# Seven block products for eight blocks of each FFN: gate weight sums on VectorE, up weight sums on GpSimd

## What is computed

```python
D_MODEL = 1024
SEQ = 512
D_FF = 2816

def swiglu_ffn(x, gain, w_gate, w_up, w_down):
    h = rms_norm(x, gain)
    return (jax.nn.silu(h @ w_gate) * (h @ w_up)) @ w_down
```

## Time and profile before

| | |
|---|---|
| median of 3 runs | 1033.64 us (1031.59 to 1034.01) |
| span of the profiled execution | 1029.8 us |
| PE busy | 1020.8 us, 5674 matmuls |
| PEld busy | 841.4 us |
| DVE busy | 545.6 us |
| ACT busy | 367.5 us |
| POOL busy | 386.1 us |
| PE clock granted | 0.999 |
| HBM read | 92.16 MB |

### The profile page before, as it was taken

The page is one execution under the profiler, slowest core; times in us unless marked ns, Lnnn a source line. Parts: engine busy times, 40 slices in busy tenths (PEclk is TensorE's granted clock), DMA queues, the critical chain, the costliest instruction groups (busy, mean ns, idle before and its releaser), DMA issues.

```text
span 1029.8 us, 14318 instructions
## 1 busy us (share of the span) xinstructions
PE 1020.8 (99%) x5674; PEld 841.4 (82%) x5674; DVE 545.6 (53%) x839; ACT 367.5 (36%) x503; POOL 386.1 (37%) x97
## 2 busy tenths in 40 slices
PE   9999999999999999999999999999999999999998
PEld 7878888888888888788877888888888888888887
DVE  5593344433444477862557884784333443344435
ACT  7533213222132243444356664632321322213220
POOL 0164433434434431533252201526353443443440
PEclk9999999999999999999999999999999999999999
DMA  8333222232232221231221001313323223222212
GB/s 320 126 123 122 82 101 103 81 119 85 81 118 86 89 115 41 88 117 41 83 78 48 3 2 41 123 41 123 123 81 116 87 81 122 81 88 116 81 41 82
DMA packets 15734, 94.80 MB, mean 92 GB/s; under 512 B 2000, under 2 KB 2128, under 8 KB 5456
## 3 DMA queue, kind: packets, MB, share of 16 engines
q1 hardware_dynamic: 15696, 94.27, 25.4%
HBM read 92.16 MB, written 2.10 MB: 92 GB/s over the span
## 4 chain that ended last, share of the span: by engine, by line
PE 91%; DVE 4%; DMA 1%; issue 1%; ACT 1%; POOL 1%; SPq 1%; POOLq 0%; DVEq 0%
PE bank L1497 83%; DMA raw<-stream 1%; POOL wlo L387 1%; PE bank L1851 0%; DVE prob L1255 0%; PE bank L1855 0%; DVE rowmax L1257 0%; PE bank L1899 0%; ACT sqx L477 0%; DVE alo L874 0%; PE bank L1782 0%; PE bank L1965 0%; PE bank L1877 0%; PE bank L1801 0%; PE bank L1954 0%
## 5 line engine op out<-in xcount | busy, mean ns | idle before, releaser
L387 POOL TENSOR_TENSOR wlo<-raw,whi 128x2048 fp32r<-128x2048 f32 x80 | 370.1, 4629 | 548.0 <-ACT whi L452 534.7
L1497 PE MATMUL bank<-ahi,whi 128*128 128x512 f32 x944 | 370.6, 393 | 2.2 <-POOL wlo L387 2.2
L1497 PE MATMUL bank<-ahi,wlo 128*128 128x512 f32 x944 | 367.7, 389 | 0.0
L1497 PE MATMUL bank<-alo,whi 128*128 128x512 f32 x944 | 367.4, 389 | 0.0
L452 ACT ACTIVATE whi<-raw 128x2048 fp32r<-128x2048 f32 x80 | 152.6, 1912 | 339.9 <-PE bank L1497 315.9
L1497 PEld LDWEIGHTS bank<-ahi,whi 128*128 128x128 f32 x944 | 177.2, 188 | 42.5 <-POOL wlo L387 2.6
L1497 PEld LDWEIGHTS bank<-ahi,wlo 128*128 128x128 f32 x944 | 177.2, 188 | 37.1
L1497 PEld LDWEIGHTS bank<-alo,whi 128*128 128x128 f32 x944 | 177.3, 188 | 35.9
L1017 DVE SCALAR_TENSOR_TENSOR x<-bank,x 128x512 f32<-128x512 f32 x176 | 120.9, 690 | 83.8 <-PE bank L1497 83.2
L1497 PE MATMUL bank<-hhi,whi 128*128 128x512 f32 x352 | 137.2, 390 | 0.0
L1497 PE MATMUL bank<-hlo,whi 128*128 128x512 f32 x352 | 137.0, 389 | 0.0
(11 more groups left out here) (277 smaller groups left out, 739.1 us busy)
## 6 DMA issues: line engine op xcount, KB each, us to landing
raw<-stream SPq DMA_DIRECT2D x80, 1024.0 KB, 4.7
raw<-stream SPq DMA_DIRECT2D x6, 512.0 KB, 6.5
x<-x_in SPq DMA_DIRECT2D x4, 512.0 KB, 7.2
out<-x SPq DMA_DIRECT2D x8, 256.0 KB, 2.0
raw<-stream SPq DMA_DIRECT2D x4, 256.0 KB, 6.5
memx<-mem_in SPq DMA_DIRECT2D x2, 512.0 KB, 10.6
cst<-const_in SPq DMA_DIRECT2D x1, 480.0 KB, 7.3
cst<-const_in SPq DMA_DIRECT2D x1, 256.0 KB, 5.7
```

What stands on the lines that cost most here:

```text
L387: nc.gpsimd.tensor_tensor(wlo[:, u % RING, :], raw[:, u % RAW, :], whi[:, u % RING, :].bitcast(F32), ALU.subtract).then_inc(w_lo, 1)
L1497: ins = E.matmul(dst, a, b, start=(n == 0 and i == 0), stop=(n == last and i == 2))
```

## The change

The first three blocks of each FFN (CLASSIC = 3) stay as they were; the other eight (FAST = 8, `i` from 0 to 7, called bodies here) get gate and up by seven products. The 1024x256 weight block is cut into four blocks of 512x128, and the input into four blocks of 512 channels x 256 tokens. Each of gate and up is then seven products (items q = 0 to 13 of a body; 0 to 3 gate, 4 to 7 up, 8 to 10 gate, 11 to 13 up) of 4x3 = 12 matmuls with 256 moving columns. Down is as before, 48 matmuls of 512 columns.

What comes with it:

- Input side, once per FFN, during the three classic blocks: DVE writes the normalized x (`normalize`, 8 instructions of 128x512), four differences (`t_total`, 128x1024) and six low parts (`t_low`, 128x1024); ACT seven high parts (`t_high`, 128x1024); POOL one low part. Three pairs of the operands lie in the place of `ahi` and `alo` and are written only once the last classic up unit is through.
- Weight side, per body: the sums of weight blocks are one add of 128x1024 and two of 128x512 for gate on DVE (`weight_sums`) and the same for up on POOL (`up_sums`). ACT makes 18 high pieces of 128x512 in groups of one to four (`pieces_high`), POOL 14 low pieces of 128x512 one at a time (`piece_low`), DVE the four low pieces of the down unit as one instruction of 128x2048 (`down_low`). The rings are used as 12 slots of such pieces.
- Output side, per body: for gate and up each, ACT copies 128x256 out of PSUM (`p6_copy`), DVE makes three combinations of 128x256 (`combine`) before the last three products and two (`fix`) after them. The scaling by the norm is gone from the bodies, since the input is normalized.
- Waits: item 8 waits for `combine` of gate and item 11 for `combine` of up (`c22_done`); the DMA of a body's gate weights waits for low piece 10 of the body before, that of its up weights for piece 13, that of its down weights for `down_low`. `weight_sums` of the next body stands between the two `combine` on DVE (in body 0 behind both).
- The loops are written out. In the mixing part, `weight_hi(U_IN + 1)` on ACT moves from before `x_parts(1)` to behind it. In FFN1, ACT makes the high part of unit v+1 before the first silu, and DVE the second half of the first hidden block behind the memory sums.

```diff
+            def first_four(f, i, g):
+                q, xb, yb = 4 * g, 2 * g, 2 * g + 1
+                seventh(f, i, q, T_B11, xb, 0, True, g == 0 and i > 0)
+                seventh(f, i, q + 1, T_1, yb, 0, True, False)
+                seventh(f, i, q + 2, T_3, yb, 1, False, False)
+                seventh(f, i, q + 3, T_2, xb, 1, False, False, four_done)
+            def last_three(f, i, g):
+                q, xb, yb = 8 + 3 * g, 2 * g, 2 * g + 1
+                pe.wait_ge(c22_done, 2 * (FAST * f + i) + g + 1)
+                seventh(f, i, q, T_B21, xb, 0, False, False, x_bank_done)
+                seventh(f, i, q + 1, T_4, yb, 1, False, False)
+                seventh(f, i, q + 2, T_B22, yb, 0, False, False, y_bank_done)
...
+                for i in range(FAST):
+                    h = n0 + 2 * (i + CLASSIC)
+                    if i == 0:
+                        pe.wait_ge(gate_scaled, 2 * CLASSIC * (f + 1))
+                    else:
+                        pe.wait_ge(silu_done, h)
+                    first_four(f, i, 0)
+                    pe.wait_ge(h_done, h)
+                    first_four(f, i, 1)
+                    last_three(f, i, 0)
+                    last_three(f, i, 1)
+                    pe.wait_ge(f_down_lo, (FAST + 1) * f + i + 1)
+                    pe.wait_ge(h_lo, h)
+                    fast_down(f, BODY * i + 14, (i + CLASSIC - 1) % 2, d0 + KD * (i + CLASSIC - 1))
```

DVE, classic part and bodies:

```diff
+                hidden(f, 0)
+                normalize(f)
+                gate_scale(f, 1)
+                t_total(f, T_1)
+                t_total(f, T_3)
+                t_low(f, T_B11)
+                t_low(f, T_1)
+                ffn_add(d0, 0)
+                ffn_add(d0, 1)
+                hidden(f, 1, low=False)
+                for d in range(2, KD):
+                    ffn_add(d0, d)
+                hidden_low(f, 1)
+                t_low(f, T_3)
+                weight_sums(f, 0, 0)
+                gate_scale(f, 2)
+                t_total(f, T_2)
...
+                t_total(f, T_4)
+                hidden(f, 2, low=False)
+                t_low(f, T_B21)
+                ffn_add(d0 + KD, 4)
+                ffn_add(d0 + KD, 5)
+                t_low(f, T_B22)
+                ffn_add(d0 + KD, 6)
+                ffn_add(d0 + KD, 7)
+                t_low(f, T_4)
+                hidden_low(f, 2)
+                for i in range(FAST):
+                    before = d0 + KD * (i + CLASSIC - 1)
+                    combine(f, i, 0)
+                    if 0 < i < FAST - 1:
+                        weight_sums(f, i + 1, 0)
+                    combine(f, i, 1)
+                    if i == 0:
+                        weight_sums(f, 1, 0)
+                    down_low(f, i)
+                    fix(f, i, 0)
+                    fix(f, i, 1)
+                    ffn_add(before, 0)
+                    ffn_add(before, 1)
+                    fast_hidden(f, i)
+                    ffn_add(before, 2)
+                    ffn_add(before, 3)
+                    fast_hidden_low(f, i)
```

POOL and SP, per body:

```diff
+            def ffn_low(f):
+                for i in range(FAST):
+                    for q in range(POOLED):
+                        if q == 4:
+                            up_sums(f, i)
+                        piece_low(f, i, q)
...
+                    for g in range(2):
+                        if i == 0:
+                            sp.wait_ge(w_lo, U_SECOND[f] + 5 + g)
+                        else:
+                            sp.wait_ge(f_lo, POOLED * (FAST * f + i - 1) + (11, 14)[g])
+                        fast(f, i, g)
```

ACT, per body:

```diff
+                    pieces_high(f, i, 10, 1)
+                    pieces_high(f, i, 11, 2)
+                    pieces_high(f, i, 13, 1)
+                    p6_copy(f, i, 0)
+                    pieces_high(f, i, 14, 4)
+                    if 0 < i < FAST - 1:
+                        pieces_high(f, i + 1, 0, 1)
+                    p6_copy(f, i, 1)
...
+                    fast_silu(f, i, 0)
+                    if i < FAST - 1:
+                        pieces_high(f, i + 1, 1, 3)
+                    fast_silu(f, i, 1)
```

More of the change, by code:

```diff
@@ L51 @@
 EARLY = 4
+HALF = T // 2
+K2 = KD // 2
+PIECE = 512
+SLOTS = RING * 4
+CLASSIC = 3
+FAST = FG - CLASSIC
+BODY = 18
+POOLED = 14
+USED = BODY * FAST + 3
+LAST_DOWN = BODY * FAST + 4
+(T_B11, T_1, T_3, T_2, T_B21, T_B22, T_4) = range(7)
 C_ID, C_UP, C_ONE, C_NEG, C_LEV = 0, P, 2 * P, 3 * P, 4 * P
@@ L399, in masks @@
+            for u in range(EARLY, U_IN):
+                split(u)
+            ffn_low(0)
             def masks(pair, l):
@@ L432, in _ @@
             pool.wait_ge(pv_done, 2 * NM)
[L433 to L437, removed]
+            for u in range(U_OUT + 2, UNITS):
+                split(u)
+            ffn_low(1)
         @block.scalar
@@ L523, in ffn_last @@
                 for a in range(2):
[L524 to L548, removed]
@@ L551, in _, with t_high @@
-            with act.Fori(0, FG // 2) as j:
-                ffn_pair(0, j)
-            ffn_last(0, (U_IN, U_IN + 1))
+                    act.wait_ge(h_done, 2 * FG * f + 2 * unit + a + 1)
+                    A.activation(hhi[:, 2 * (unit % 2) + a, :], gbuf[:, a, :], ACT.Copy).then_inc(h_hi, 1)
+            def t_high(f, j):
+                if j == T_B11:
+                    act.wait_ge(xn_ready, KD * f + K2)
+                elif j in (T_1, T_3, T_2):
+                    act.wait_ge(t_sum, 4 * f + j)
+                elif j == T_4:
+                    act.wait_ge(t_sum, 4 * f + 4)
+                else:
+                    act.wait_ge(xn_ready, KD * f + KD)
+                    act.wait_ge(w_used, U_SECOND[f] + 5)
+                A.activation(tt[f][j][0][:], t_source(f, j), ACT.Copy).then_inc(t_hi, 1)
@@ L1583, in up_tile, with down @@
                 return i.then_inc(done, 1)
-            def down(u, b, free, last=False):
+            def down(u, b, free):
                 for d in range(KD):
-                    if d >= 4 or last:
-                        pe.wait_ge(x_added, free + (d - 3))
+                    if free + d - 3 > 0:
+                        pe.wait_ge(x_added, free + d - 3)
                     for k in range(2):
@@ new lines, in seventh @@
+            def seventh(f, i, q, j, bank, h, start, fresh, done=None):
+                pe.wait_ge(f_lo, POOLED * (FAST * f + i) + q + 1)
+                if i == 0:
+                    if j == T_2:
+                        pe.wait_ge(t2_lo, f + 1)
+                    else:
+                        pe.wait_ge(t_lo, 6 * f + (j if j > T_2 else j + 1))
+                (at, _), = places(BODY * i + q, 1)
+                hi, lo, _ = tt[f][j]
+                for k in range(K2):
+                    w = tuple(in_ring(part, at + k * P, P) for part in (whi, wlo))
+                    for m, (a, b) in enumerate(((w[0], hi), (w[0], lo), (w[1], hi))):
+                        ins = E.matmul(psum[bank][:, HALF * h:HALF * (h + 1)], a, b[:, k, :],
+                                       start=start and k == 0 and m == 0, stop=k == K2 - 1 and m == 2,
+                                       skip_group_check=True)
+                        if k == 0 and m == 0:
+                            ins.then_inc(f_used, 2 if fresh else 1)
+                if done is not None:
+                    ins.then_inc(done, 1)
```

452 lines of the change are left out of this document (364 added, 88 removed).

## The result

The changed kernel takes 1036.56 us (median of 9 runs, 1033.76 to 1041.54), the kernel before 1032.04 on the same chip (9 runs): a ratio of 1.0041, 95% interval 1.0022 to 1.0060. So it is slower by 0.4%, where 1024 was forecast, faster by 1%. Spans of the profiled executions: 1033.0 after, 1029.8 before.

The account below looks back on a forecast made before the run. PE's matmul stream was taken as the bound: 33.6 us saved, less (8 - 2.2), 4.4, 9.4, 1.5 and 14 x 0.2 lost, gives 9.7 less: span 1020.1, median 1023.9, told as 1024; forecast's range 1008 to 1036, overall 1001 to 1050.

Parts of the forecast that it names:

- loop in steady state: Steady bodies: DVE and POOL turns delay `combine` of up for item 11, losing about 0.2 us per body, 14 bodies.
- FFN1 to mixing: Passage from FFN1 to mixing: POOL's 4.6 us falls between DVE's sums, PE's statistics wait, 1.5 us lost.
- What bounds it: Whole kernel: PE's matmul stream is the time, PE busy 1020.8 of 1029.8 us; other engines have room.
- What it removes: Gate and up of 16 bodies: 256-column matmuls at 0.1170 us each save 2.1 us per body, 33.6 us in all.
- Rival C: All bodies: a 256-column matmul costs 0.1204 us, 9 us less gain, 1033 us, no change; chance 0.05.
- The exclusion: Bodies: DVE instructions with both inputs in SBUF and POOL's run only in turns, filling 28.6 of 30.5 us.
- rival B: Steady bodies: DVE and POOL turns close a longer loop, 2.5 us per body for 14 bodies, 1059 us; chance 0.22.
- Start of the FFNs: First classic blocks: late additions to x cost 8 us in FFN1, 4.4 in FFN2; an old 2.2 us wait goes.
- Body 0: First body of each FFN: DVE's load delays item 8 by 3.8 us, body 1 some 0.9; 9.4 in both FFNs.
- Rival A: Whole kernel: PE bound throughout, waits overlap better, only about 4 us lost, 1002 us; chance 0.18.

Follow-up runs that it names:

- the best kernel: Changed kernel with T_4 ahead of the additions, first additions ahead of normalizing, and all bodies' next gate sums queued behind `down_low`: 1005.63 us, ratio 0.9734.

## Why the prediction was wrong

**Sum, term by term** (minus is time saved; after against before):

| term | forecast | measured |
|---|---|---|
| 16 bodies, matmuls of 256 columns | -33.6 | -25.3 |
| start of FFN1, old stall gone | +5.8 | +5.0, and +1.1 before the first gate |
| start of FFN2 | +4.4 | +2.5 |
| body 0 and 1, both FFNs | +9.4 | +20 |
| loop in steady state | +2.8 | 0 |
| FFN1 to mixing | +1.5 | 0 |
| sum | -9.7 | +3.3 (spans: +3.2) |

The +1.1 before the first gate is not of the change: PE reaches the first sums of squares at 31.28 before and at 32.41 here, and between 30.97 and 32.45 in the other orders of the changed kernel, whose work up to there is the same.

**What bounds it.** Right: PE's stream is the time, the steady bodies are pure PE, and nothing costs more there than the matmuls.

**What it removes: the step that failed first.** The price of 256 columns was the line through 512 and 264 columns, 0.1170, and the step said that a load "does not set the pace" because loads of 188 ns come every 0.12 us. That is no argument: they overlap, so their duration says nothing of how fast they can follow each other. Measured is 0.1199, all but the 0.1204 of the nearest row. Rival C had this price and was given 0.05. The 8.3 us that this step gave too much stand beside the 10.6 of body 0 below; the other terms give 6 back.

**The exclusion** was right in kind and near in size: POOL's low pieces last 1.42 us on average (1.515 those of the sums, 1.33 the others) where they take 1.28 alone, and POOL is busy for 26 of 31 us, its turns of waiting counted. It did not close the loop: in the body that starts at 221.4 the combination of up ends 14.7 us in and item 11 is due at 15.8, so 1.1 us are to spare, where the walk had lost 0.2. The run with longer sums shows that it was the right loop to fear (rival B's mechanism) and that its edge is about 1 us away. B's time needed 2.5 us per body.

**Start of the FFNs.** The walk was right almost row by row: normalizing was put at 56.9 to 70.7 and ran from 56.73 for 14.10 us; the first addition at 77.4 came at 76.61; PE waited for exactly that, and the 2.20 us of the earlier trace rows are gone. The 8 us were 7.5, but for a partly different reason: 4.82 of wait, not 8, and the rest slow matmuls behind it, for which the prediction had no term. That the sum nearly came out is luck. In FFN2 PE waited 2.36 us where 4.4 was walked.

**Body 0: the step that failed most.** It had a wait of 3.8 at item 8, by DVE's load. DVE was about as late as walked: it has the gate half combined at 131.74, 13.8 us into the body (15.0 in the walk, due at 11.2), but PE had been held at item 4 by then and did not wait for it. Three things were missed. The walk had POOL at its up sums before DVE made T_4, but they stand behind T_2's low part, which waits for T_4: the piece of item 4 came late, 2.2 us. The walk of body 0 ended at item 8; `down_low` was walked in the steady loop alone (ready at 17.8), and in body 0 it stands behind the gate sums of body 1 and is ready at 28.2: 3.9 us. And behind each wait PE ran slowly, 3.7 us more. Of the three, two are places in a queue behind a wait that the waiting work doesn't need, which the order of the calls in the diff shows; the runs with T_4 first and with the sums behind confirm both.

**FFN1 to mixing.** POOL's unit did meet DVE there (an instruction of DVE lasted 5.5 us), but PE's statistics did not wait for it: 0 in place of 1.5.

**Rivals and range.** The result, 1036.6, is in the range, but past the forecast's own 1008 to 1036 and on the side that had a chance of 0.23. It lies near rival C's 1033, for C's price and some 4 us more of stalls than C had from the forecast. Rival A's 1002, PE bound throughout, is what the same instructions reach in a better order: 1003.6.

## What to carry to other kernels

Take the price of a narrower matmul from the nearest width that the trace has, not from a line: the gain per column ends where the load of the stationary operand sets the pace. When a change puts a wait for a landing into an engine's queue, list what stands behind it and when each of these is due; the work without a near deadline goes last. Walk the first bodies of a pipeline by themselves, and price a stall of PE of some us at up to twice its length, for the clock can come down with it.

## What the hardware showed

- **The clock behind short waits.** Waits of 4.82, 2.22 and 3.89 us in the changed kernel were followed by windows of 4.7 to 5.9 us with mean granted clocks of 0.50 to 0.71. A wait of 2.36 in FFN2 was not, nor was the 2.20 of the earlier trace rows (windows behind these two, of the changed kernel and of the kernel before):

```profile
724.93:731.00 6.07, 6.07 (x27) 4.99 (x27) 5.38 (x9) 1.93 (x2) 0.69 (x1) 1.00 0.18 74
```

```profile
57.33:63.00 5.67, 5.67 (x25) 4.69 (x26) 5.63 (x4) 0.75 (x1) 4.96 (x1) 1.00 0.52 185
```

  The length of the wait doesn't tell: at the same place in FFN2 the kernel with T_4 first has a wait of 2.35 with a clock of 0.75 behind it (first window), the one with `down_low` first a wait of 2.35 with none (second). What does tell stays open.

```profile
723.25:730.00 6.75, 6.75 (x22) 5.38 (x23) 4.54 (x8) 1.82 (x2) 0.00 (x0) 0.75 0.17 73
```

```profile
731.41:738.00 6.59, 6.59 (x29) 5.46 (x30) 5.92 (x9) 1.93 (x2) 1.25 (x1) 1.00 0.16 67
```

- **A toss between DVE and POOL.** Near the end of FFN1 `down_low` and POOL's 2048-column low part start within 0.03 us of each other. In one execution (first timeline, longer sums in the best kernel) DVE takes 6.70 us and four additions to x wait behind it, which costs PE 3.85; in another (second timeline, the best kernel) POOL takes 6.79 and nobody waits:

```profile
355.48 6.70 DVE L1287 TENSOR_TENSOR wlo<-raw_down,whi 128x2048 fp32r<-128x2048 f32 x1
355.45 4.58 POOL L472 TENSOR_TENSOR wlo<-raw,whi 128x2048 fp32r<-128x2048 f32 x1 [13.01 <-ACT whi L577]
```

```profile
355.59 2.29 DVE L1285 TENSOR_TENSOR wlo<-raw_down,whi 128x2048 fp32r<-128x2048 f32 x1
355.56 6.79 POOL L472 TENSOR_TENSOR wlo<-raw,whi 128x2048 fp32r<-128x2048 f32 x1 [17.31 <-ACT whi L577]
```

  All twelve profiled executions of the changed kernel and its other orders have this meeting, 0.02 to 0.03 us apart. POOL's lasts longer in seven, the changed kernel's among them, and PE has no such wait; DVE's in five (`down_low` first, sums behind for bodies 1 and 2 and for 1 to 3, and both with longer sums), and in each of these five PE waits 3.85 or 3.86 for an addition to x and the clock is at 0.50 for a while. Four of these five took the longest or next to the longest time of their kernel's runs, the fifth 1011.1 where the fastest took 1006.3. That this meeting makes the spread of 5 to 9 us between runs of some kernels, and the two groups of the changed one, is likely and not shown, for one execution of each kernel was profiled.
- **Landings.** 1 MB took 4.9 us by the page's median, but 6.7 us at one place where a chain hung on it.
